# Operand tiles moved to other byte offsets in SBUF, and a last norm with tokens on the partitions

## The reference, cut to what matters

```python
def rms_norm(x, g):
    x32 = x.astype(jnp.float32)
    y = x32 * lax.rsqrt(jnp.mean(x32 * x32, axis=-1, keepdims=True) + EPS)
    return (y * g.astype(jnp.float32)).astype(x.dtype)
...
def swiglu(h, w1, w3, w2):
    return (jax.nn.silu(h @ w1) * (h @ w3)) @ w2
...
        x = x + g_f * swiglu(modulate(rms_norm(x, norm_ffn[l]), sh_f, sc_f),
                             w_ffn1[l], w_ffn3[l], w_ffn2[l])
    return rms_norm(x, final_norm)
```

## Time and profile before

| what | value |
|---|---|
| median of 3 runs | 2059.98 us (2054.92 to 2064.69) |
| the profiled execution | 2057.38 us, span 2055.5 us |
| PE busy | 1944.1 us, 95% of the span |
| chain that ended last | PE 80%, DVE 8%, POOL 3%, ACT 3%, DMA 3% |
| POOL, DVE, ACT busy | 1114.4, 943.6, 750.2 us |
| mean granted TensorE clock | 0.964 of full |

### The profile page before, as it was taken

One profiled execution on the slowest core, in us unless ns is written; L12 is line 12 of the kernel. 1 busy time (PEld: TensorE's weight loads), 2 busy tenths in 40 slices (PEclk: granted clock), 3 DMA queues, 4 the chain that ended last, 5 costly groups with the idle time before them and its releaser, 6 DMA issues.

```text
span 2055.5 us, 33135 instructions
## 1 busy us (share of the span) xinstructions
PE 1944.1 (95%) x13903; PEld 1707.4 (83%) x13903; DVE 943.6 (46%) x1688; ACT 750.2 (36%) x1201; POOL 1114.4 (54%) x611
## 2 busy tenths in 40 slices
PE   6879999989999999999999999999999998989998
PEld 4558899977988789878777888888798997989998
DVE  7855451164554693662344111113557756373114
ACT  4333443233232722452223222222335525434442
POOL 6536677764344544344343444444368744877885
PEclk7779999999999999999999999999999999999999
DMA  7476788876213032112421323322345330555652
GB/s 148 129 253 217 258 281 270 278 253 207 83 48 106 13 113 72 62 32 92 151 85 62 103 77 108 102 80 85 96 151 154 114 104 31 192 167 159 188 164 85
DMA packets 299273, 276.19 MB, mean 134 GB/s; under 512 B 19722, under 2 KB 296724, under 8 KB 298868
## 3 DMA queue, kind: packets, MB, share of 16 engines
q1 hardware_dynamic: 296756, 270.90, 41.7%
q10 hardware_dynamic: 2048, 2.77, 0.4%
q0 software_dynamic: 320, 0.40, 0.1%
HBM read 266.18 MB, written 4.19 MB: 132 GB/s over the span
## 4 chain that ended last, share of the span: by engine, by line
PE 80%; DVE 8%; POOL 3%; ACT 3%; DMA 3%; issue 2%; SPq 1%; ACTq 0%; DVEq 0%; POOLq 0%
PE gb L2438 17%; PE gb L2439 17%; PE gb L2440 17%; PE gb L1430 4%; PE gb L1432 4%; PE gb L1431 4%; PE gb L1642 3%; POOL wl L2426 3%; PE gb L1643 3%; PE gb L1644 3%; DMA raw<-in_mlp_w 1%; PE mb L1162 1%; ACT wh L778 1%; PE mb L639 1%; PE mb L1229 1%
## 5 line engine op out<-in xcount | busy, mean ns | idle before, releaser
L2426 POOL TENSOR_TENSOR wl<-raw,wh 128x1024 fp32r<-128x1024 f32 (+3 forms) x452 | 982.2, 2191 | 841.2 <-ACT wh L778 840.9
L778 ACT CAST wh<-raw 128x1024 fp32r<-128x1024 f32 (+3 forms) x452 | 418.4, 937 | 746.8 <-PE gb L2440 363.1
L2438 PE MATMUL gb<-xh,wh 128*128 128x256 f32 (+1 forms) x1856 | 605.3, 326 | 14.9 <-DVE xl L1111 6.7
L2440 PE MATMUL gb<-xh,wl 128*128 128x256 f32 (+1 forms) x1856 | 601.0, 324 | 0.0
L2439 PE MATMUL gb<-xl,wh 128*128 128x256 f32 (+1 forms) x1856 | 600.7, 324 | 0.0
L2438 PEld LDWEIGHTS gb<-xh,wh 128*128 128x128 f32 x1856 | 353.2, 190 | 53.9 <-issue 14.7
L2440 PEld LDWEIGHTS gb<-xh,wl 128*128 128x128 f32 x1856 | 352.5, 190 | 28.0
L2439 PEld LDWEIGHTS gb<-xl,wh 128*128 128x128 f32 x1856 | 352.9, 190 | 27.5
L1430 PE MATMUL gb<-wh,xh 128*128 128x256 f32 x608 | 174.4, 287 | 1.4 <-POOL wl L2426 1.3
L1431 PE MATMUL gb<-wh,xl 128*128 128x256 f32 x608 | 172.7, 284 | 0.0
L1432 PE MATMUL gb<-wl,xh 128*128 128x256 f32 x608 | 172.7, 284 | 0.0
(11 more groups left out here) (451 smaller groups left out, 2946.9 us busy)
## 6 DMA issues: line engine op xcount, KB each, us to landing
raw<-in_w_in SPq DMA_DIRECT2D x62, 1024.0 KB, 5.4
raw<-in_w_ada SPq DMA_DIRECT2D x48, 1024.0 KB, 6.4
raw<-in_w_ffn SPq DMA_DIRECT2D x44, 1024.0 KB, 5.1
raw<-in_mlp_w SPq DMA_DIRECT2D x32, 1024.0 KB, 5.3
raw<-in_w_ffn SPq DMA_DIRECT2D x16, 768.0 KB, 4.6
raw<-in_w_ffn SPq DMA_DIRECT2D x16, 640.0 KB, 4.3
raw<-in_ssm_w_glu SPq DMA_DIRECT2D x8, 1024.0 KB, 6.9
raw<-in_w_out SPq DMA_DIRECT2D x8, 1024.0 KB, 5.1
```

What stands on the lines that cost most here:

```text
L778: nc.scalar.copy(split_half(wh, p, j, h), raw_half(p, it, j, h)).then_inc(hi_ready, 1)
L2426: nc.gpsimd.tensor_tensor(split_half(wl, p, j, h), raw_half(p, it, j, h), split_half(wh, p, j, h).bitcast(F32), ALU.subtract)\
L2438: nc.tensor.matmul(o, H[:, k, :], XH, start=st, stop=False)
L2440: return nc.tensor.matmul(o, L[:, k, :], XH, start=False, stop=sp_)
```

## The change

Two independent things. First, the offsets: all operands that are read with 512 columns start at a multiple of 512 bytes, and most of those that are read with 256 columns start 160 bytes (40 floats) beyond one, high and low part at the same offset. `brh`, `brl`, `dqTh`, `dqTl`, `fhh`, `fhl` now start at 0, and their columns are shifted by 40 floats where T is 256 (`home("layer", T)`); norms 0, 1 and 7 shift `xh` and `xl` by 40 floats; `hidl`, `pth`, `ptl` move to 160 as `hidh`. The gated projection (`"glu"`) now reads 0 and 0, and the 256-column reads of the 512-column norm of the last layer (n = 5) stay at 0 and 0. The instructions on all engines are the same there, with other addresses.

Second, the last norm. PE transposes each finished residual tile during the last `ffn2_pe`, two transposes per tile, one block late; tiles 6 and 7 follow after the last block. The result, tokens on the partitions, lies in PSUM. ACT squares it there with a running sum per token (columns 0 to 511 within the stream, the other 384 and 128 after the end), DVE makes the reciprocal root of two numbers per partition, and scales from PSUM straight to `onat` with `grow`, the gain, which a DMA broadcasts to all partitions at the start of the last `ffn2`. Four stores of 256 KB (ACT and SyncE in turn) replace two of 512 KB. Gone are the sums over partitions, the diagonal and its spreading, the in-place scaling, the ACT copies, and the unused products of that norm.

```diff
-        beside(part_m, 224)
+        beside(part_m, 160)
         hidl = part_m("hidl", [P, FF1 // P, SEQ], F32R)
...
+        beside(part_p, 160)
         pth = part_p("pth", [P, 2, SEQ], F32R)
...
-        beside(part_2, 128)
+        beside(part_2, 0)
...
-        beside(part_2, 64)
+        beside(part_2, 0)
         brh = part_2("brh", [P, 4, SEQ + CTX], F32R)
-        beside(part_2, 256)
+        beside(part_2, 0)
         brl = part_2("brl", [P, 4, SEQ + CTX], F32R)
...
-        beside(z3, 16)
+        beside(z3, 0)
         dqTh = z3("dqTh", [P, 4, SEQ + CTX], F32R)
-        beside(z3, 448)
+        beside(z3, 0)
...
-        beside(part_h, 320)
+        beside(part_h, 0)
         fhl = part_h("fhl", [P, FH, SEQ + CTX], F32R)
...
-        HOME = {"glu": (0, 16), 0: (16, 32), 1: (64, 80), 7: (4, 40)}
-
-        def home(n, e, T):
-
-            o = HOME[n][e] if n in HOME else 0
+        HOME = {0: 40, 1: 40, 7: 40, "layer": 40}
+
+        def home(n, T):
+
+            o = HOME.get(n, 0) if T == SEQ else 0
             return slice(o, o + T)
...
-                        XH, XL = fhh[:, k, 0:T], fhl[:, k, 0:T]
+                        XH, XL = fhh[:, k, home("layer", T)], fhl[:, k, home("layer", T)]
...
+        def final_transposes(it, j):
+
+            p = L2[LAYERS - 1]["f2", 1]
+            i = 4 * it + j
+            for k in ([i - 1] if i else []) + ([KD - 1] if i == KD - 1 else []):
+                wait_drained(nc.tensor, p, k // 4, k % 4, 1)
+                for a in range(2):
+                    dst = gb[:, 1, a * P:a * P + P] if k == KD - 1 else mb[:, 2 * a + k // 4, (k % 4) * P:(k % 4) * P + P]
+                    ins = nc.tensor.transpose(dst, x[:, k, a * P:a * P + P], ident)
+                if k in (3, 6, 7):
+                    ins.then_inc(s_ot, 1)
...
+                if half and l == LAYERS - 1:
+                    act.wait_ge(s_fl, FL[l][half])
+                    act.dma_start(grow[:, :], A["final_norm_2"].partition_broadcast(P)).then_inc(s_gain, 16)
+                    gemm_act(act, q["f2", half], final_squares)
...
+        def final_view(a, part):
+
+            return (mb[:, 2 * a, :], mb[:, 2 * a + 1, 0:3 * P], gb[:, 1, a * P:a * P + P])[part]
...
+        def square_final_part(part):
+
+            nc.scalar.wait_ge(s_ot, part + 1)
+            for a in range(2):
+                if part + a:
+                    nc.scalar.wait_ge(s_oc, 2 * part + a)
+                src = final_view(a, part)
+                nc.scalar.activation(osq[:, 0:src.shape[1]], src, ACT.Square, accum_out=fsum[:, a, part:part + 1])\
+                    .then_inc(s_oc, 1)
...
-            norm_pe(pe, 8, sqr2, dg2)
-            pe.wait_ge(s_res, RES_END)
-            for a in range(2):
-                for k in range(KD):
-                    ins = nc.tensor.transpose(mb[:, 2 * a + k // 4, (k % 4) * P:(k % 4) * P + P],
-                                              x[:, k, a * P:a * P + P], ident)
-                ins.then_inc(s_ot, 1)
...
-            norm_dve(dve, D1, 8, vec(V_FIN2), sqr2, dg2, in_place=True)
-            dve.sem_inc(s_res, 1)
+            dve.wait_ge(s_oc, 6)
+            total = rs[:, 3, 0:2]
+            step(v.tensor_reduce(total, fsum[:, :, :], AX_X, ALU.add))
+            step(v.tensor_scalar(rs[:, 0, 0:2], total, 1.0 / D, EPS, ALU.mult, ALU.add))
+            rsqrt_beside(D1, rs[:, 0, 0:2], rs[:, 1, 0:2], gb[:, 3, 448:450], gb[:, 3, 456:458], last=rs[:, 2, 0:2])
+            dve.wait_ge(s_gain, 16)
+            for a, h in FINAL:
+                for part in range(h, 2 * h + 1):
+                    src = final_view(a, part)
+                    c = (0, 512, 512 + 3 * P)[part]
+                    cs = slice(c, c + src.shape[1])
+                    ins = v.scalar_tensor_tensor(onat[:, a, cs], src, rs[:, 2, a:a + 1], grow[:, cs], ALU.mult, ALU.mult)
+                    if part == 1:
+                        D1.add(ins)
+                if h:
+                    D1.wait()
+                ins.then_inc(s_on2, 1)
```

More of the change, by code:

```diff
@@ L657, in build, with final_store @@
         block = ctx.enter_context(nc.Block())
+        FINAL = [(a, h) for a in range(2) for h in range(2)]
+        def final_store(eng, n):
+            a, h = FINAL[n]
+            eng.wait_ge(s_on2, n + 1)
+            hs = slice(512 * h, 512 * h + 512)
+            eng.dma_start(out[0, a * P:(a + 1) * P, hs], onat[:, a, hs]).then_inc(s_out, 16)
         @block.sync
@@ L730, in _ @@
                 load(sp, g)
-            sp.wait_ge(s_out, 16 * 2)
+            for n in range(1, len(FINAL), 2):
+                final_store(sp, n)
+            sp.wait_ge(s_out, 16 * 4)
         def unit_view(p, j, T):
@@ L1105, in norm_dve @@
                     for i, part in enumerate(parts(T)):
-                        here = [home(n, e, T) if T == SEQ else part for e in range(2)]
-                        src, hi, lo = ring[:, (k - 1) % 4, part], xh[:, k - 1, here[0]].bitcast(F32), xl[:, k - 1, here[1]]
+                        here = home(n, T) if T == SEQ else part
+                        src, hi, lo = ring[:, (k - 1) % 4, part], xh[:, k - 1, here].bitcast(F32), xl[:, k - 1, here]
                         if shift is None:
@@ L1625, in back_pe, with ffn2_pe @@
             ins.then_inc(s_ott, 1)
-        def ffn2_pe(pe, p, T, pairs):
+        def ffn2_pe(pe, p, T, pairs, after=None):
             def turn(it):
@@ L1646, in turn @@
                             ins.then_inc(mm_done, 1)
+                    if after is not None:
+                        after(it, j)
             for it in range(p.n // p.body):
@@ L1717, in mixed_hi @@
                     act.wait_ge(s_mx, 4 * l + k // 2 + 1)
-                    nc.scalar.mul((brh if k < 4 else xh)[:, k, 0:T], mix[:, k, 0:T], 0.5).then_inc(s_mh, 1)
+                    nc.scalar.mul((brh if k < 4 else xh)[:, k, home("layer", T)], mix[:, k, 0:T], 0.5).then_inc(s_mh, 1)
             def before(it, j):
@@ L1772, in back_act @@
             for f in range(4):
-                nc.scalar.activation(dqTh[:, f, 0:T], mb[:, f, 0:T], ACT.Copy, scale=dgain[:, l:l + 1])\
+                nc.scalar.activation(dqTh[:, f, home("layer", T)], mb[:, f, 0:T], ACT.Copy, scale=dgain[:, l:l + 1])\
                     .then_inc(s_brh, 1)
@@ L2146, in layer_dve @@
                             t = t0 + 4 * it + j
[L2147 to L2148 removed]
+                            v.scalar_tensor_tensor(fhl[:, t:t + 2, home("layer", T)], two(pr2, s_, T), 0.5,
+                                                   fhh[:, t:t + 2, home("layer", T)].bitcast(F32),
                                                    ALU.mult, ALU.subtract).then_inc(s_fl, 1)
[L2150 removed]
+                scaled_residual(q["f2", half], 40, 1, lambda p, j, i: unit_view(p, j, T),
+                                half == 1 and l < LAYERS - 1)
             D1.wait()
@@ L2319, in _ @@
                 layer_act(act, l)
-            for a in range(2):
-                act.wait_ge(s_ot, a + 1)
-                nc.scalar.copy(onat[:, a, :], mb[:, 2 * a:2 * a + 2, :].rearrange("p b n -> p (b n)")).then_inc(s_oc, 1)
-                act.wait_ge(s_oc, a + 1)
-                act.dma_start(out[0, a * P:(a + 1) * P, :], onat[:, a, :]).then_inc(s_out, 16)
+            square_final_part(1)
+            square_final_part(2)
+            for n, (a, part) in enumerate(FINAL):
+                if n % 2 == 0:
+                    final_store(act, n)
         @block.gpsimd
```

77 lines of the change are left out of this document (38 added, 39 removed).

## The result

The changed kernel takes 2045.91 us (median; 2041.48 to 2051.18), the kernel before, run beside it, 2055.94 us: ratio 0.9948, 95% interval 0.9933 to 0.9963. (One further execution took 2667.44 us at a mean granted clock of 0.66 and is left out of the ratio.) By the ratio that is some 10.7 us faster. The interval excludes a ratio of 1, and it reaches to both sides of 0.5%. The profiled execution took 2041.48 us.

What follows compares the result with a forecast made beforehand. PE was taken to bound the kernel (80% of the chain). Gains of 6.5 (512 columns), 1.3 (256 columns) and 2.8 (tail), less 0.8 for waits, made 9.8 us: from the median 2060.0 to 2050.2 us, range 2041 to 2058.5.

Steps and rivals of the forecast that it cites:

- the 512-column one: Feed-forward, branches and output projection: moving 512-column operands to offset 0 gains 6.5 us, slow `xh` matmuls included.
- the 256-column one: 1312 triples moved to 160 and 160 take 353.7 ns instead of near 354.7, 1.3 us gained.
- the tail's: Last norm: 4.1 us gained after the last residual tile, 1.35 lost to transposes in PE's stream, net 2.8 us gained.
- The slow `xh` matmuls behind a switch: Branches and output projection: `xh` matmuls after `brh` or `dqTh` blocks lose their 5.8 ns excess, 0.8 us taken as gain.
- the deduction: Among the branches, waits take back part of what faster matmuls give; 0.8 us subtracted.
- Rival 1: 160 and 160 is the best place for 256 columns: all triples at 351.2 ns, 3.3 us more gained, 2047; chance 0.13.
- rival 2: 256 columns: equal high and low offsets cost 120 ns, not offset 0; 7.0 us lost there, 2058.5 us; chance 0.11.
- Rival 4: 160 is a bad start for long 256-column reads: triples at 376.5 ns, 20 us slower, 2080; chance 0.04.
- rival 3: All moved operands: the address plays no part in the pace, only the tail gains, 2057 us; chance 0.08.

Runs made afterwards that it cites:

- the kernel with 192: The changed kernel with every 256-column operand that was at 160 bytes moved to 192; 2038.43 us, ratio 0.9925 to the kernel before.

## Why the prediction came out right

**The total.** 9.8 us were forecast, 10.0 by the medians and 10.7 by the ratio came. The forecast of 2050.2 us lies 4.3 us over the 2045.91 measured, because it started from a median of three executions, 2059.98, and ten gave 2055.94. The change was forecast at 0.53 to stay within 0.5%, close to the line, and at 0.52% it lies on it. Of its three terms the 512-column one is right in size, the 256-column one by luck, and the tail's a little too small in its gain.

**512 columns: right, with its size.** 16.5 and 17.4 ns per triple were forecast; `fhh` went to 680.0 ns from 696.6, `brh` and `dqTh` to 680.0 and some 681 from 699.6 (the 697.5 of the earlier trace rows was the lower end of theirs). The feed-forward gave 2.8 us (2.9). The slow `xh` matmuls behind a switch are gone: 12 `brh` matmuls and the `xh` behind them run at 226.7. Between 204 and 1074 us the pair gained 7.2, of which 2.0 are the clock at 1042; the 5.2 left are to be set against 2.8 + 0.8 and some 0.3 from 256-column triples of the first block, less 0.8 for waits. Measured by the triples, `brh` and `dqTh` gave 3.1 and the `xh` between them 0.5 (682.3 to 680.2 ns). So the 5.2 are more than the terms give even without the deduction. The other 1.3 us are not explained; the mean granted clock of that stretch, 0.980 before and 0.986 after, may hold them. Among the branches PE's idle time grew by 2 us (18.4 to 20.5), between 204 and 1074 us it did not (28.5 and 28.3), so the runs don't tell whether the deduction was needed. The reason I gave, a start that is a multiple of 512 bytes, was too narrow: 256 does as well, and what counts is the distance to the weights.

**256 columns: right on average, by luck of the neighbour row.** 353.7 was taken; measured were 352.2 in norm 7 to some 355 and 357 in `dqTh` and the output projection. Weighted by their numbers the 1312 triples go from 354.7 to 353.7 ns, the 1.3 us forecast. But in the offsets-alone kernel norm 7 and the last `fhh` showed 356.0, and the same sum gives 0.7 us lost: the same offsets differ by 4 ns from program to program, more than the term itself (1.0 ns). One operand did not move as the change was told: in the grouped-query branch of the last layer `brh` is read without the shift, so its 32 triples went to 0 and 0 and from 356.2 to 360.0 ns, 0.1 us lost. Rival 1 (351.2) was almost met in norm 7, rival 2 is refuted as a rule (equal offsets of 160 don't cost) yet right about 0: the kernel with everything at 0 has 360 nearly everywhere. Rival 4 (376.5) and rival 3 (no part of the address) are out. The Trainium skill's page "TensorE: Matmul & The Clock Gate", section "Wait — 56ns, not 53.3ns?", gives N / 2.4 GHz + 2.5 ns for a warm stream, with no term for the address: 215.7 ns at 512 columns and, an estimate by that formula, 109.2 ns at 256. The traces here do not agree with it: the steady stretches never ran below 226.7 and 113.3 ns per matmul, and the address moves them up to 234 and 120.

**The tail: right, its end costed 0.8 us too dear.** 12.1 us were forecast, 11.3 measured, piece by piece: from the residual tile to DVE's chain 2.65 (forecast 3.1), the chain 3.19 (3.2), the scalings 2.97 (3.0), from there to the end 2.5 (2.8). The squares were faster than costed (0.49 + 0.19 for 384 columns against 0.58 + 0.20, 0.28 + 0.20 for 128 against 0.35 + 0.20), and so was the landing. A pair of transposes in the stream costs 0.23 us in the kernel with the tail alone and 0.25 by the rows of the kernel with 192 (the triple ahead of it takes 0.48 and the next 0.45 instead of 0.34 each), 1.35 to 1.5 for six pairs against 1.35 forecast; that they also switch the pace of the triples behind them I had not foreseen.

**The median and the profiled pair.** The profiled execution of before lay below its median, and so did that of after (2041.48 against 2045.91). The pair shows 15.8 us; stretches at half clock that fall elsewhere in each execution go with 2.9 + 2.0 - 1.6 = 3.3 of the 5.8 us that it shows beyond the medians. The 2.9 among them rests on the mean clock alone.

## What to carry to other kernels

Read a matmul stream's pace from start to start per operand, and sort it by the distance between the starts of the moving and the stationary operand modulo 256 bytes; here 512 columns wanted 0, and 256 columns wanted 192 and shunned 0. Then measure, since the same distance did not always give the same pace. If the activation must serve both widths, move the weights per stage instead. Compare medians for the total and the same instructions for the places: a single pair of profiles here was off by 5.8 us, more than half of the effect.

## What the hardware showed that I had not expected

- The pace depends on both operands: for 256 columns 120.0 ns at distance 0, 113.3 or 117.8 at 192 and, with the weights moved, at 64, mostly 116.7 to 119 elsewhere (120 in some blocks at 32); for 512 columns 226.7 at 0, 229 at 64 with the weights moved, 233 to 234 elsewhere. At 2.4 GHz 226.7 and 113.3 ns are 544 and 272 cycles, columns times 17/16, and 120.0 is 288. Why, is open: no run separates a bank of the memory from the reads of the weight load, which runs beside each matmul.
- At 192, and at 64 with the weights moved, there are two lasting paces, 340 and 353 ns per triple. At 192 two transposes can switch between them, in both directions. What picks one wasn't found; a stream kept at 340 throughout wasn't tried.
- Distance 96 gave 360.0 as well, with only 32 triples in one execution; I don't rest anything on it.
- Four stores of 256 KB issued within 0.8 us land in 2.0 to 3.2 us, spread over 2.2 us in 2.0 to 2.1.
